# Second half of the output projection placed between the join steps of the first mixer stage

## What is computed

```python
    o_a, s_gdn_new = gated_delta_chunked(q, k, v, beta, logd, s_gdn)
    o_a = rms_norm(o_a, p['gdn_norm_w']).reshape(bsz, L, A_VAL) * jax.nn.silu(z_a)
    ...
    o_b = (o_b * p['rwkv_ln_w'] + p['rwkv_ln_b'] + bonus) * jax.nn.silu(gb)
    y = jnp.concatenate([o_a, o_b], axis=-1).astype(x.dtype) @ p['w_out0']
    return x + y, conv_new, s_gdn_new, xn[:, -1], s_rwkv_new
```

## Time and profile before

| what | us |
|---|---|
| time, median of 3 runs | 2095.77 (2094.67 to 2101.37) |
| the profiled execution | 2099.86 |
| its span in the profile | 2098.2 |
| PE busy | 1814.6 (86%) |
| DVE busy | 852.3 (41%) |
| ACT busy | 501.5 (24%) |
| POOL busy | 311.3 (15%) |
| mean granted clock of PE | 0.867 |

### The profile page before, as it was taken

The page is one execution under the profiler, slowest core; times in us unless marked ns, Lnnn a source line. Parts: engine busy times, 40 slices in busy tenths (PEclk is TensorE's granted clock), DMA queues, the critical chain, the costliest instruction groups (busy, mean ns, idle before and its releaser), DMA issues. The chain is left out here.

```text
span 2098.2 us, 32158 instructions
## 1 busy us (share of the span) xinstructions
PE 1814.6 (86%) x13399; PEld 1583.5 (75%) x13399; DVE 852.3 (41%) x1454; ACT 501.5 (24%) x907; POOL 311.3 (15%) x266
## 2 busy tenths in 40 slices
PE   3999969999738988898888885899999996999985
PEld 3899959889627766876668664799999995777764
DVE  4255543655444465546665533300100103443432
ACT  4244432333301121211212022321111112111101
POOL 3322211112020111111112001211111102000000
PEclk6999989999957788779888975999999996788887
DMA  5122221321162322333234013423123104432215
GB/s 142 31 84 84 84 64 42 105 97 45 50 214 56 79 61 59 88 81 83 66 95 88 20 31 104 134 94 93 42 63 104 42 22 162 121 100 74 70 51 46
DMA packets 248647, 166.27 MB, mean 79 GB/s; under 512 B 90994, under 2 KB 230491, under 8 KB 248520
## 3 DMA queue, kind: packets, MB, share of 16 engines
q1 hardware_dynamic: 248520, 164.44, 28.3%
HBM read 106.51 MB, written 57.89 MB: 78 GB/s over the span
## 5 line engine op out<-in xcount | busy, mean ns | idle before, releaser
L1775 PE MATMUL c_bank<-c_wo,c_ot 128*128 128x512 f32 (+1 forms) x288 | 144.7, 667 | 8.5 <-ACT c_ot L1351 8.3
L2360 DVE SCALAR_TENSOR_TENSOR e_t<-e_t,e_bank 128x512 f32<-128x512 f32 (+1 forms) x20 | 12.7, 633 | 289.7 <-ACT e_t L2313 289.7
L1775 PEld LDWEIGHTS c_bank<-c_wo,c_ot 128*128 128x128 f32 (+1 forms) x288 | 59.4, 210 | 89.2 <-issue 80.3
L85 PE MATMUL e_bank<-e_wp0h,e_xh 128*128 128x256 f32 x432 | 123.2, 285 | 1.8 <-issue 1.8
L87 PE MATMUL e_bank<-e_wp0h,e_xl 128*128 128x256 f32 x432 | 123.0, 285 | 0.0
L86 PE MATMUL e_bank<-e_wp0l,e_xh 128*128 128x256 f32 x432 | 122.9, 285 | 0.0
L85 PE MATMUL e_bank<-e_wp1h,e_xh 128*128 128x256 f32 x432 | 122.3, 283 | 0.0
L86 PE MATMUL e_bank<-e_wp1l,e_xh 128*128 128x256 f32 x432 | 122.3, 283 | 0.0
L87 PE MATMUL e_bank<-e_wp1h,e_xl 128*128 128x256 f32 x432 | 122.2, 283 | 0.0
L85 PEld LDWEIGHTS e_bank<-e_wp0h,e_xh 128*128 128x128 f32 x432 | 83.7, 194 | 2.1 <-issue 2.0
L86 PEld LDWEIGHTS e_bank<-e_wp0l,e_xh 128*128 128x128 f32 x432 | 83.7, 194 | 0.0
(11 more groups left out here) (570 smaller groups left out, 4774.6 us busy)
## 6 DMA issues: line engine op xcount, KB each, us to landing
k_w<-in_w_in_dram SPq DMA_DIRECT2D x33, 512.0 KB, 6.2
e_w<-in_w_in_dram SPq DMA_DIRECT2D x16, 1024.0 KB, 6.7
scratch_rw<-b_x SPq DMA_DIRECT2D x16, 544.0 KB, 2.7
c_rw<-scratch_rw SPq DMA_DIRECT2D x32, 256.0 KB
scratch_qkv<-a_o SPq DMA_DIRECT2D x12, 544.0 KB, 5.5
e_xs<-scratch_xnT SPq DMA_DIRECT2D x8, 544.0 KB, 3.8
scratch_ql<-e_qb SPq DMA_DIRECT2D x8, 544.0 KB, 3.0
n_x<-in_x_prompt_dram SPq DMA_DIRECT2D x8, 512.0 KB, 3.7
```

Source lines behind the costliest of these rows:

```text
L85: pe.matmul(out, w[0], x[0], start=first, stop=False)
L1775: mm = pe.matmul(bank[e[c]][0:T, :], OT[:, kt, 0:T], wo[:, kt, 512 * c:512 * c + 512], start=(kt == 0), stop=(kt == KT - 1))
L2360: dve.scalar_tensor_tensor(out=t2, in0=t2, scalar=1.0, in1=two(b, at), op0=ALU.add, op1=ALU.mult).then_inc(ev(f"free{b}"), 1)
```

## The change

PE's `end_project` keeps only the first half (c = 0) where both halves stood. The eight products of the second half go into the four fills: one at the end of fill 1, two in fill 2, two in fill 3, three in fill 4. DVE's `end_add` moves from behind the transpose that opens join 4 to behind the eviction of z5, and `end_mean` from behind the transposes of join 5 to behind the eviction of z6. ACT's `end_square` moves from behind the copy of y4 to behind `rh`. The sample tile's pass is as it was. No product and no transfer is added or taken away.

```diff
@@ scalar engine
                     act.activation(Y4[:, :, :], vu(2, SUB, 0, UNITS), ACT.Copy).then_inc(ev("y4"), 1)
-                    if i:
-                        end_square(i - 1, P)
...
                     rh(i, P, a1)
+                    if i:
+                        end_square(i - 1, P)
@@ vector engine
                     turn(XT4[:, :, :], X5[:, :, :], "xt4")
-                    if i:
-                        end_add(i - 1, P, e)
                     dve.wait_ge(ev("z4mm"), n)
...
                         turn(XF[q32(q), :, q32(q)], X5[q32(q), :, :], "xf5")
-                    if i:
-                        end_mean(i - 1, P)
...
                     dve.tensor_scalar(X6[32:64, :, 0:32], vu(1, 32, 0, UNITS)[32:64], -1.0, None, ALU.mult).then_inc(ev("z5"), 1)
+                    if i:
+                        end_add(i - 1, P, e)
                     wr(i, P, a0)
...
                     dve.tensor_scalar(XF[0:64, 6:UNITS, 64:128], vu(3, 64, 0, 6)[0:64], -1.0, None, ALU.mult).then_inc(ev("xf6b"), 1)
+                    if i:
+                        end_mean(i - 1, P)
                     nv(i, P)
@@ tensor engine
-                    for kt in range(KT):
+                    project_steps(T, e, c, range(KT))
+
+                def project_steps(T, e, c, kts):
+                    for kt in kts:
                         mm = pe.matmul(bank[e[c]][0:T, :], OT[:, kt, 0:T], wo[:, kt, 512 * c:512 * c + 512],
                                        start=(kt == 0), stop=(kt == KT - 1))
-                    mm.then_inc(ev("prj"), 1)
+                        if kt == KT - 1:
+                            mm.then_inc(ev("prj"), 1)
...
                         end_rows(i - 1, P, e)
-                        for c in range(2):
-                            end_project(i - 1, P, e, c)
+                        end_project(i - 1, P, e, 0)
+
+                    def second_half(kts):
+                        if i:
+                            project_steps(P, e, 1, kts)
...
                     def fill1():
                         ks(range(AH))
+                        second_half((0,))
 
                     def fill2():
                         kd((0, 1))
+                        second_half((1, 2))
 
                     def fill3():
                         kd((2,))
+                        second_half((3, 4))
 
                     def fill4():
                         kd((3,))
+                        second_half((5, 6, 7))
```

## The result

The changed kernel takes 2111.93 us (median of 20 runs, 2107.52 to 2119.93), the kernel before 2101.18 (20 runs, 2086.35 to 2115.82). The ratio is 1.0054, 95% interval 1.0036 to 1.0072: slower by about 11 us. Slower was forecast, but by 66 us, and 2111.93 lies outside the range.

The account below looks back on a forecast made before the run. PE was taken as the bound, busy 86% of the span, often below full clock, its projection covering the DRAM way. Terms summed to +9.5 us a pass, +66.5 for seven, on 2099.86: 2166, median 2162; range 2124 to 2188.

Parts of the forecast that it names:

- y4 starts at the landing: Ahead of the joins: y4 starts when X5 lands, no longer behind the projection; -1.2 us a pass.
- joins' own work: From y4 to y6: work already there slows because y4 starts at half clock; +2.1 us a pass, bound +2.9.
- eight products: In the four fills: the moved products are paid whole, half clock for five and mostly for three; +11.0 us a pass.
- y6 to L1782: From y6 to the normed rows' transposes: clock more often full after three wide products, 15.0 for 17.48; -2.5 us a pass.
- moved steps: DVE's sums and mean and ACT's square at their new places: nearly free; +0.1 us a pass, at worst +0.5.
- The clock: Joins, fills and solve: 5.9 us idle puts y4 at half clock, which returns late in the fills; +2.1, +11.0, -2.5 a pass.
- Rival 1: In the fills: clock returns early, in fill 2, and stays up; +4.2 us a pass, +29 in all, 2125 us; chance 0.17.
- wait of 5.9 us ahead of y4: Ahead of y4: PE idles from the first half's end at 765.4 until `ld_x5` at 771.3, released by the DMA.
- half clock at y4: At y4's start: after 5.9 us without work the granted clock is 0.50 in the seven passes.
- nothing for the products to hide behind in the fills: In the fills: evictions are already covered, so products stand in line; at best 1.0 us a pass off, counted as nothing.
- the order of DVE and ACT without a new wait: Around y6: sums, `wr` and square fit the cover ahead of y6's eviction and z6's copy; square 0 to 0.3 us.
- they are for the next pass ... and cost nothing: SP's queue: loads of q, k, v start later, about 1 us into y6, needed over 15 us later; no cost.

Follow-up runs that it names:

- all eight in fill 1: Changed kernel with all eight products of the projection's second half in fill 1: 2109.62 us, ratio 1.0026 to the kernel before.
- run with the wait filled: Changed kernel plus six needless products per pass in PE's wait ahead of y4, their result overwritten: 2100.22 us, ratio 1.0002 to the kernel before.
- loads late: Kernel before with only SP's loads of q, k and v for the next tile issued behind the eviction of z5: 2085.49 us, ratio 0.9937.
- steps moved only: Changed kernel with all 16 products back ahead of y4; DVE's sums and mean and ACT's square stay moved: 2090.03 us, ratio 0.9959 to before.
- seven ahead: Changed kernel with seven of the second half's products ahead of y4 and the last in fill 4: 2079.93 us, ratio 0.9912 to before.
- six ahead: Changed kernel with six of the second half's products ahead of y4, one in fill 3 and one in fill 4: 2076.04 us, ratio 0.9893 to before.
- all in fill 4: Changed kernel with all eight products of the second half in fill 4: 2143.92 us, ratio 1.0180 to the kernel before.
- wait at 750 filled: On top of seven ahead, three needless wide products in PE's 3.3 us wait ahead of the rows' transposes: 2127.71 us, ratio 1.0111 to before.
- before, three extra: Kernel before plus three needless products of the projection's form at the end of fill 4 in seven passes: 2105.65 us, ratio 1.0024.
- five ahead, spread: Changed kernel with five of the second half's products ahead of y4, one each in fills 2, 3 and 4: 2087.19 us, ratio 0.9923 to before.

## Why the prediction was wrong, step by step

The terms of one pass, as forecast and as measured in the changed kernel:

| term | forecast | measured |
|---|---|---|
| y4 starts at the landing | -1.2 | -1.0 |
| joins' own work (10.50 before) | +2.1 | -1.3 |
| eight products | +11.0 | +8.2 |
| y6 to L1782 (17.48 before) | -2.5 | -5.0 |
| moved steps | +0.1 | within the rows above |
| sum | +9.5 | +0.9 |

The step that failed is the one headed "The clock": "I take half clock for the first five and mostly for the last three, with some passes earlier: +11.0 for the eight", with the +2.1 and the -2.5 that hang on it. The clock was back ahead of fill 2 in six of seven passes, with the first product of eight at half clock or partly so, and stayed up through all seven solve stretches. I had one stretch as the measure of its return, the 5.58 us of the earlier trace rows, and compared the runs in the fills with it one by one, as if each had to do it alone. The traces show it back sooner than that: the clock rose while the first product ran in three passes, and all eight in fill 1 had it back after 2.2 us on average, against 4.2 in fill 4. Why it is shorter there, whether by `ks` right ahead or by something else, stays open. From the start of each run to the start of what follows, the eight products took 8.2 us a pass (7.7 to 8.9), not 11.0, and the joins' own work the other 9.2, not 12.6. It is even less than the 10.50 of before: PE has no waits there any more (7.0 us before) and is at full clock behind fill 2, where in four passes before it was at half.

Rival 1, at 0.17, came closest to this mechanism, and its time of 2125 was still 13 us high, or 18 when its +29 is set against the measured +11. It priced the own work at 11.0 (+0.5, where -1.3 was measured) and the products at 9.6; the solve stretch it had right (-4.7 for -5.0).

That slower came true is in part luck. The terms nearly cancel (+6.9, -5.0, -1.0), and half of the 12 us between the two profiled spans arises outside the changed passes.

What held: the wait of 5.9 us ahead of y4 and its releaser, half clock at y4 in all seven passes, nothing for the products to hide behind in the fills (PE is busy for 121.69 of 121.70 us), the order of DVE and ACT without a new wait of more than 0.4 us. The Trainium skill, "TensorE: Matmul & The Clock Gate", section "HAM oscillation — how this bites in real kernels", has a loop that pauses for a transfer in each round begin each round at half clock. The trace of the changed kernel agrees (0.50 at y4 behind the 5.86 us), and so does the run with the wait filled (1.00 there, and 11 us less).

A second step failed and is hidden in the sum: "they are for the next pass ... and cost nothing", said of SP's loads. That is true of their lateness, but their absence from the joins is a gain: loads late, which moves nothing else, is 0.6% faster than before, and steps moved only 0.4%. I had counted nothing for the 7.0 us of PE's waits in the joins, since they have no releaser. So the +0.54% is the sum of two changes: the moved steps -0.41%, and the split of the projection, which costs the rest, 1.0054 / 0.9959 = 1.0095, some 20 us or 2.9 a pass. Of that, the run with the wait filled gives back 11 by the clock alone, without any useful work back in the wait.

Why six or seven ahead are best is, in the main, argued from this: PE arrives at the landing with at most 1.2 us to wait, next to no cover is lost, the clock at y4 is full, the loads are out of the joins, and five solve stretches of seven run at full clock. In the two or three other passes the clock still falls in the joins or behind them. Which passes these are differs between kernels, and the time of one kernel scatters (2072 to 2084 for six ahead); only one execution of each was profiled, so what is chance in the number of such passes is open.

## What to carry to other kernels

Move products out of a wait's cover only as far as PE then just meets the landing; what is beyond it stands in line, and all that can come back of its price is what it does for the clock behind it. Price PE's work at the clock of its stretch, and ask of every piece of wide work what it does to the clock of what follows: here 21 useless products cost 5 us and not 18, and filling a 3 us wait cost 42 to 48. When a step of one engine moves, look at the queues behind it, also for what their transfers stop disturbing.

## What the runs showed of the hardware

- PE busy is not what lifts the granted clock. At 0.50 it stayed there through 13.22 us of joins with PE busy throughout (32 x 32 products, `ks` and `kd`), and rose within the 9.24 us of eight 128 x 512 products (all in fill 4, i = 2). The Trainium skill, "TensorE: Matmul & The Clock Gate", Part 1, has the clock follow how busy the array has been; by the profile's busy time these rows do not agree.
- Narrow work lost the clock with no wait ahead of it: in the kernel before it fell from 1.00 to 0.50 in six passes of seven, with no idle time of PE over 1.3 us since y4, and the solve stretch took 17.6 to 18.6 us for 12.80. With waits of 2.4 to 3.0 us ahead of y4 it fell in seven passes of seven (wait at 750 filled, solve stretch 17.94); with waits of 0 to 1.2 us the solve stretch lost it in two of seven (six and seven ahead).
- Three 128 x 512 products right ahead of y6 had the clock at 1.00 for the whole solve stretch in seven passes of seven (before, three extra: 12.08 us for 17.48), also where they themselves ran mostly at half clock.
- With a DMA share of 0.36 to 0.52 beside the joins PE had 1.0 us a pass of waits without a releaser (before), with 0.14 to 0.19 it had 0.6 (loads late). The loads are not the only cause: with 0.02 it still had 0.4 (steps moved only), 0.5 (seven ahead) and 0.9 (five ahead, spread), and none in the changed kernel.
